# HGRN2 score tiles of a hybrid decoder step: the blocks of the two upper levels put into the plain product's tile, and a buffer of their own for the second prompt tile's prefix queries

## The reference

```
S_t = diag(f_t) S_{t-1} + k_t v_t^T ;   o_t = S_t^T q_t
```

```
score[s, t] = sum over k of  q[t,k] * exp(G[t,k] - G[s,k]) * k[s,k]     for s <= t
o[t] = sum over s of score[s, t] * v[s]  +  (q[t] * exp(G[t])) @ S(at the tile's start)
```

## Time and profile before

| | us |
|---|---|
| median of 3 runs | 1782.69 |
| the 3 runs | 1782.69, 1788.0, 1781.02 |
| span of the profiled execution | 1779.5 |
| PE busy | 1707.1 (96%) |
| DVE busy | 1295.3 (73%) |
| ACT busy | 1039.2 (58%) |

### The profile page before, as it was taken

How to read it: one execution, slowest core, us unless ns; L and a number is a source line. 1 busy time by engine, 2 the same in 40 slices (tenths; PEclk the granted TensorE clock), 3 DMA queues, 4 the chain that set the end, 5 groups by cost and what they waited for, 6 DMA issues and landing times.

```text
span 1779.5 us, 23283 instructions
## 1 busy us (share of the span) xinstructions
PE 1707.1 (96%) x9626; PEld 1490.1 (84%) x9626; DVE 1295.3 (73%) x1111; ACT 1039.2 (58%) x942; POOL 95.4 (5%) x85
## 2 busy tenths in 40 slices
PE   8999889999999988789999999999999999999997
PEld 7988778999999977678888888888888888788886
DVE  6636655444347356739988888888898888888897
ACT  4444333333334344237777777777777777777776
POOL 2000120000000010302300000000000000000200
PEclk9998989999999989899999999999999999999999
DMA  9559154443553512248999999999999999999994
GB/s 300 166 163 266 43 156 135 142 154 103 147 168 119 166 41 69 53 165 315 393 393 398 395 366 390 374 382 395 364 381 373 368 398 392 316 394 368 375 392 186
DMA packets 272617, 474.21 MB, mean 266 GB/s; under 512 B 41578, under 2 KB 103266, under 8 KB 272504
## 3 DMA queue, kind: packets, MB, share of 16 engines
q1 hardware_dynamic: 266432, 452.50, 71.5%
q10 hardware_dynamic: 3368, 12.75, 2.2%
q0 software_dynamic: 2704, 7.39, 1.4%
HBM read 454.82 MB, written 29.84 MB: 272 GB/s over the span
## 4 chain that ended last, share of the span: by engine, by line
PE 87%; DVE 7%; issue 2%; ACT 2%; DMA 1%; DVEq 0%; ACTq 0%; SPq 0%
PE ps L1709 16%; PE ps L1710 16%; PE ps L2344 11%; PE ps L1704 9%; PE ps L1705 9%; PE ps L2365 5%; PE ps L1803 4%; PE ps L2230 3%; PE ps L1911 2%; PE ps L2248 1%; DVE spL L1589 1%; PE ps L2383 1%; PE ps L2192 1%; PE ps L1896 1%; DMA ring<-in_w_exp_in_dram 1%
## 5 line engine op out<-in xcount | busy, mean ns | idle before, releaser
L1589 DVE TENSOR_TENSOR spL<-ring,spH 128x2048 fp32r<-128x2048 f32 x336 | 767.3, 2292 | 99.2 <-ACT spH L964 96.6
L964 ACT ACTIVATE spH<-ring 128x2048 fp32r<-128x2048 f32 x336 | 643.0, 1916 | 129.5 <-PE ps L2344 70.2
L1709 PE MATMUL ps<-spH,XH 128*128 128x512 f32 x896 | 354.1, 395 | 1.8 <-issue 1.8
L1710 PE MATMUL ps<-spH,XL 128*128 128x512 f32 x896 | 349.9, 391 | 0.0
L1047 DVE TENSOR_TENSOR spL<-ring,spH 128x2048 fp32r<-128x2048 f32 (+1 forms) x74 | 158.8, 2146 | 182.3 <-ACT spH L659 182.2
L1704 PE MATMUL ps<-hnH,spH 128*128 128x320 f32 x928 | 277.8, 314 | 4.0 <-DVE hnL L1062 2.2
L1705 PE MATMUL ps<-hnL,spH 128*128 128x320 f32 x928 | 276.2, 312 | 0.0
L659 ACT ACTIVATE spH<-ring 128x2048 fp32r<-128x2048 f32 (+1 forms) x74 | 133.4, 1803 | 188.4 <-PE ps L2230 73.6
L2344 PE MATMUL ps<-spL,XH 128*128 128x512 f32 x896 | 241.4, 391 | 0.9 <-DVE spL L1589 0.9
L2344 PEld LDWEIGHTS ps<-spL,XH 128*128 128x128 f32 x896 | 168.6, 188 | 37.6 <-DVE spL L1589 1.8
L1709 PEld LDWEIGHTS ps<-spH,XH 128*128 128x128 f32 x896 | 168.6, 188 | 36.1 <-issue 2.2
(11 more groups left out here) (362 smaller groups left out, 1802.9 us busy)
## 6 DMA issues: line engine op xcount, KB each, us to landing
ring<-in_w_exp_in_dram SPq DMA_DIRECT2D x224, 1024.0 KB, 8.4
ring<-in_w_exp_out_dram SPq DMA_DIRECT2D x112, 1024.0 KB, 8.3
ring<-in_w_in_dram SPq DMA_DIRECT2D x28, 1024.0 KB, 5.3
ring<-in_w_ffn_in_dram SPq DMA_DIRECT2D x22, 1024.0 KB, 5.1
token_rows<-token_rows ACTq DMA_DIRECT2D x1, 11776.0 KB, 42.5
ring<-in_w_ffn_out_dram SPq DMA_DIRECT2D x16, 704.0 KB, 4.6
ring<-in_w_out_dram SPq DMA_DIRECT2D x8, 1024.0 KB, 5.1
out_dram<-ring SPq DMA_DIRECT2D x32, 256.0 KB, 2.7
```

The lines of the kernel that those rows point to most:

```text
L964: A(esplit(j)[0], src, ACT.Copy).then_inc(S("hi_done"), 1)
L1589: V.tensor_tensor(lo, eslot(j)[0], hi.bitcast(F32), ALU.subtract).then_inc(S("split_done"), 1)
L1709: mm(out, x[0], w, start=start, stop=False)
L1710: return mm(out, x[1], w, start=False, stop=False)
```

## The change

The number of levels that have a tile of their own becomes `LOW` = 5 for the prompt tiles. The plain product takes the sixth place. Into that tile PE then writes, over the plain product, the blocks of levels 5 and 6, and only the blocks: two of 32 x 32 and one of 64 x 64. The mask table shrinks from 8 to 6 tiles, the last one keeping the diagonal and both levels' blocks. `masked` covers 768 columns where it covered 1024, and `output` sums six tiles where it summed eight. `exponents`, `decays` and Yk are as they were.

`products` makes Yq for the levels alone (128 x 896 in prompt tiles). For tile 1 it makes the prefix queries by an instruction of their own into the new buffer `qGp`, which has a place for each head and lies where SS lies; L1916 reads it there. Every head now waits for `scores` of the head two before, and none for its `output`. In layer 1 a wait for the store of SS stands ahead of the first write of `qGp`. In the sample tile nothing changes but that Yq no longer has its prefix block, which is not read from there.

```
+LOW = 5
-        "mask": mp.reshape(P, -1)
+        "mask": np.concatenate([mp[:, :LOW], mp[:, LOW:].sum(1, keepdims=True)], 1).reshape(P, -1)
+        qGp = put("qGp", [P, H, P], offset=cursor[0] - 4 * NH * HD)
...
 products:
                     dve.wait_ge(S("x_exp"), j + 1)
-                    if t == 1 and h >= 2:
-                        dve.wait_ge(S("o_mm"), j - 1)
-                    elif j >= 2:
+                    if j >= 2:
                         dve.wait_ge(S("sc_mm"), j - 1)
-                    q_b = qT[:, h, o:o + n].unsqueeze(1).broadcast_to([P, nl + 1, n])
+                    q_b = qT[:, h, o:o + n].unsqueeze(1).broadcast_to([P, nl, n])
-                    V.tensor_tensor(Yqv, Mv, q_b, ALU.mult)
+                    V.tensor_tensor(Yqv[:, 0:nl], Mv[:, 0:nl], q_b, ALU.mult)
                     if t == 1:
+                        if l and h == 0:
+                            dve.wait_ge(S("ssp_stored"), 16 * l)
+                        V.tensor_tensor(qGp[:, h], Mv[:, nl], qT[:, h, o:o + n], ALU.mult)
                         own(V.tensor_copy(egp[:, h:h + 1], Mv[:, nl, n - 1:n]))
...
 masked:
-                        V.tensor_tensor(SCv, ps[:, 2:4, :].rearrange("p b n -> p (b n)"), tabv("mask"), ALU.mult
+                        V.tensor_tensor(SCv, ps[:, 2:4, :].rearrange("p b n -> p (b n)")[:, 0:(LOW + 1) * n], tabv("mask"),
...
 scores:
-                    for v in range(nl + 1):
-                        out = ps[0:n, 2 + (v * n) // 512, (v * n) % 512:(v * n) % 512 + n]
-                        if v < nl:
+                    full = LOW if t < 2 else nl
+                    for v in range(full + 1):
+                        at_ = (v * n) % 512
+                        out = ps[0:n, 2 + (v * n) // 512, at_:at_ + n]
+                        if v < full:
...
+                    for v in range(full, nl):
+                        b = 1 << v
+                        for s0 in range(0, n, 2 * b):
+                            m = mm(ps[s0:s0 + b, 2 + (full * n) // 512, at_ + s0 + b:at_ + s0 + 2 * b],
+                                   flat(Ykb[h % 2])[:, v * n + s0:v * n + s0 + b],
+                                   flat(Yqb[h % 2])[:, v * n + s0 + b:v * n + s0 + 2 * b], start=True, stop=True)
...
 output:
-                    for v in range(nl + 1):
+                    top = LOW if t < 2 else nl
+                    for v in range(top + 1):
...
-                        m = mm(out, SH[:, h * P:(h + 1) * P], flat(Yqb[h % 2])[:, nl * n:(nl + 1) * n],
-                               start=False, stop=True)
+                        m = mm(out, SH[:, h * P:(h + 1) * P], qGp[:, h], start=False, stop=True)
```

More of the change, by code:

```diff
@@ L87, in constants @@
         "w": wp.reshape(P, -1), "l": lp, "ws": ws.reshape(NS, -1), "ls": lspad,
-        "id": np.eye(P), "ones": np.ones((P, P)), "mask": mp.reshape(P, -1), "ms": ms.reshape(NS, -1), "seq": seq, "turn": turn,
+        "id": np.eye(P), "ones": np.ones((P, P)),
+        "mask": np.concatenate([mp[:, :LOW], mp[:, LOW:].sum(1, keepdims=True)], 1).reshape(P, -1), "ms": ms.reshape(NS, -1), "seq": seq, "turn": turn,
         "iota": np.tile(i[None, :], (P, 1)), "before": (i[:, None] < i[None, :]),
@@ L1254, in masked @@
                         dve.wait_ge(S("o_mm"), j - 1)
-                    SCv = flat(SCb[h % 2])[:, 0:(nl + 1) * n]
+                    SCv = flat(SCb[h % 2])[:, 0:((LOW if t < 2 else nl) + 1) * n]
                     if t < 2:
-                        V.tensor_tensor(SCv, ps[:, 2:4, :].rearrange("p b n -> p (b n)"), tabv("mask"), ALU.mult
-                                        ).then_inc(S("sc_done"), 1)
+                        V.tensor_tensor(SCv, ps[:, 2:4, :].rearrange("p b n -> p (b n)")[:, 0:(LOW + 1) * n], tabv("mask"),
+                                        ALU.mult).then_inc(S("sc_done"), 1)
                     else:
@@ L1909, in output @@
                     out = ps[:, 6, h * n:(h + 1) * n]
-                    for v in range(nl + 1):
+                    top = LOW if t < 2 else nl
+                    for v in range(top + 1):
                         m = mm(out, vtk_of(t)[0:n, h * P:(h + 1) * P], flat(SCb[h % 2])[0:n, v * n:(v + 1) * n],
-                               start=v == 0, stop=v == nl and t != 1)
+                               start=v == 0, stop=v == top and t != 1)
                     if t == 1:
```

## The result

The changed kernel took 1765.93 us (median of 4 runs, 1764.86 to 1772.5) against 1782.15 (4 runs, 1781.02 to 1788.0): ratio 0.9899, 95% interval 0.987 to 0.9929. It is faster, by 16 us where 11 were forecast.

The account below looks back on a forecast made before the run. The prediction took a chain of waits through the heads, on DVE in tile 0 and alternating between PE and DVE in tile 1, as the bound. Terms of 5.48 us a layer took 11.0 off 1782.69, giving 1771.7; 8-in-10 range 1765.5 to 1780.

Parts of the forecast that it names:

- The sum of the edits: Heads of both layers: all terms together save 5.48 us a layer, 10.96 us in all.
- output: Output matmuls on PE: two of eight go, 0.51 us a head, six heads on the path, 3.06 us a layer.
- mask: Masked scores on DVE: 256 columns less, 0.267 us each, 0.80 us a layer in each of tiles 0 and 1.
- Yq: Yq on DVE: 128 columns less, 0.133 us, on the path twice in tile 0, 0.27 us a layer.
- the released wait: Tile 1, heads 2 and 3: products no longer wait for an output; 2.43 us becomes 1.93, 1.0 us a layer.
- the prefix queries: Own DVE instruction, 0.30 us a head in tile 1, covered by PE work; uncovered it would cost 2.4 us.
- The group of blocks: Scores on PE: six narrow instructions cost 0.60 us, replacing 0.45; 0.45 us a layer dearer on the path.
- Cheap blocks: Rival: blocks run side by side, group costs 0.20 us, 4 us more gained, 1767.7; shares chance 0.15 with clock gains.
- dear switches: Rival: weight-width switches make the group 1.50 us, 9 us given back, 1780.7; shares chance 0.22 with clock losses.
- blocks that don't pipeline: Rival: each block waits for the last, group 2.73 us, 10 us slower, 1792.7; shares chance 0.07 with clock falls.
- The clock rival: Clock fall at 215 to 225 us may shift: up to 3.4 us a layer either way; chances shared with other rivals.
- cheap blocks or a clock that gives something back: Branch for a time of 1764 to 1768 us, chance 0.15.

Follow-up runs that it names:

- e5: Kernel before with only the output sum cut from eight tiles to six, last level and diagonal missing from the result: mean 1777.4 us, ratio 0.9967.
- e3: Changed kernel with the wait for the output and the prefix block of Yq put back, so the blocks alone: mean 1777.0 us, ratio 0.996.
- e4: Changed kernel without the three block matmuls of each prompt head's scores, levels 5 and 6 missing from the result: mean 1761.0 us, ratio 0.9873.
- e8: Changed kernel with the group of block matmuls issued twice in a row, same result: mean 1775.4 us, ratio 0.9956 to the kernel before.
- e12: Changed kernel with the 64 x 64 block cut into two of 32 x 64, all narrow weights 32 wide: mean 1764.8 us, ratio 0.9881.
- e2: Kernel before with only the prefix queries in their own buffer and the wait for the output released: mean 1775.8 us, ratio 0.9951.
- e11: Changed kernel with the old wait for the output put back, prefix queries still in their own buffer: mean 1777.3 us, ratio 0.996 to the kernel before.
- e9: Kernel before with 17 idle-time matmuls a layer in PE's two long gaps of tile 1, nothing left out: mean 1776.6 us, ratio 0.9948.
- e6: Kernel before with 14 idle-time matmuls a layer ahead of the heads, to hold the clock: mean 1781.6 us, ratio 0.9988.
- e7: Changed kernel with 14 idle-time matmuls a layer ahead of the heads, to hold the clock: mean 1768.0 us, ratio 0.9912 to the kernel before.
- e10: Changed kernel with idle-time matmuls (8 and 4) in PE's gaps of tile 1: mean 1769.2 us, ratio 0.9899 to the kernel before.

## Why the prediction was right and wrong

*The sum of the edits* was right. 10.96 us were predicted, 10.6 to 11.3 measured at equal clock (each ± 1.2 to 1.6). Term by term, from the profile of the changed kernel: output 0.45 to 0.67 a head on the chain, 2.99 over the six of a layer (3.06 predicted; e5 gives 0.57 a head over its 12 places); mask 0.265 (0.267); Yq 0.130 (0.133); the released wait 2.43 to 1.80 (1.93); the prefix queries hidden, as SC waits for PE behind them. Summed as in the prediction, with 0.47 for the three groups that are followed by PE work, these make 5.6 us a layer, 11.3 in all. One reading in it was too simple: in tile 0 the chain of the changed kernel runs through PE at two scores before it comes back to DVE, so part of the masks' and Yq's 1.07 us there is not on the path.

*The group of blocks* was taken at 0.60 between bounds of 0.20 and 1.50. The profile has 0.44 to 0.46, and 0.12 to 0.20 on what follows where PE has work at once. My first reading after the result, that it cost 0.44 and was even with what it replaced, looked at the group's own piece of the chain and not at the next one. The next piece refutes it, and e3 and e4 lean the same way; e8 fits either, once its places are counted. The page TensorEngine Tiling (Array Packing) of the Trainium skill, Key Properties, has the engine drained at a change of mode: by that rule each change of width costs something, and the trace agrees, with the first full-width matmul after the narrow ones at 0.43 us instead of 0.23, and with e12, where one change less goes with 0.15 us less. The 0.36 us of the prediction's upper bound is seen at none of them.

*The step that failed is the clock.* The prediction put it so: "The granted clock is 1.00 through tile 1", and "in tile 1 itself PE's gaps get shorter, which speaks against a fall there". Both sentences are true of the profiled execution, and the conclusion was that this was worth nothing. But that execution was one of the better ones: its clock was 0.978, and over 73 runs the kernel before averages 0.9755. The changed kernel averages 0.9788, which took 4.3 us off the mean, a term that the sum had at nought. That this comes from the wait is shown by e2 and e11, the same wait released and kept: 0.9755 to 0.9796, and 0.9788 to 0.9734. e9 shows it from the other side, with the gaps of tile 1 filled and no edit.

How much of it is falls in tile 1 is less sure. With the wait kept and no filling, five profiles (before, e3, e5, e6, e11) have a fall in 7 of their 10 tile 1s; with it released, seven profiles (the changed kernel's two, e2, e4, e7, e8, e12) have one in 6 of 14, mostly shorter. A fall cost 2.9 us in e6, 3.2 in e3 and 1.6 in the changed kernel's profile. The lack of clock in tile 1 (length times what the granted clock is below 1.00) averages 3.7 us a profile in the first group and 1.7 in the second. That is 0.0011 of the span, where the mean clocks of the runs lie 0.0033 apart. Where the other two thirds lie, these profiles don't show.

*The rivals.* Cheap blocks, dear switches and blocks that don't pipeline did not come. The clock rival named the right thing and weighed it as chance of either sign up to 3.4 us a layer at 215 to 225 us; there a fall stays in every profile. It should have been a one-sided gain from the released wait. So the time, 1765.9, lies 5.8 us below the forecast, in the branch "cheap blocks or a clock that gives something back", which had a chance of 0.15. About 1 us of the 5.8 is luck: the four runs had a mean clock of 0.9795, the eleven 0.9788, and their means are 1767.3 and 1768.6.

*What stays open:* which share of the changed kernel's remaining loss of clock (0.0212 below 1.00) could be had; neither e7 nor e10 got any. And what e9's 7 us consist of: its clock rose by 0.0049, 8.7 us of the span, and the largest lack in tile 1 in any profile, e3's, is 6.8 us for both layers. So falls in tile 1 of the size seen here can hardly be all of it.

## What to carry to other kernels

Before a forecast from one profile, set its mean granted clock beside the clocks of the other runs; if they scatter, part of the path's price lies in falls that this profile may not show. A wait that leaves PE idle costs its length and, in some executions, half the clock for what comes next (e3: 1.7 us idle, then 3.2 us lost; e6: 2.9). A released wait can then be worth more than the chain says (e11), and a few idle-time matmuls in the gap may give the second part alone: 7 us in e9, nothing in e10, so it has to be tried. Narrow matmuls are priced with the instruction behind them, 0.15 to 0.20 us dearer here when it is full-width, and a group of one width was cheaper than one of two (e12). And when an edit is costed by dividing a time by a number of places, count the places in the chain of the kernel that was run: five were expected here, and seven or eight were found.

## What the runs showed of the hardware

Two things I had not expected. The mean granted clock orders the times of one kernel almost completely: 1.31 us per 0.001, from 1773.4 to 1790.2 us with nothing changed. And eight instructions with 32-wide weights, four with 32 columns moving and four with 64 (0.29 to 0.32 us, 0.04 each), are faster than six of which two have 64-wide weights (0.44 to 0.46): the number of instructions was not what the group cost.
